# Feed-forward projections: one 512-column matmul for the high weights, and bank halves added on the way out

## The reference, cut to what matters

```
D_FF = 2816
def swiglu(x, w_gate, w_up, w_down):
    return (jax.nn.silu(x @ w_gate) * (x @ w_up)) @ w_down

h = rms_norm(x, g_pre)
x = x + rms_norm(swiglu(h, w_gate, w_up, w_down), g_post)      # stages 4 to 12: half of it for the feed-forward blocks
```

## Time and profile before

| | us |
|---|---|
| median of 3 runs | 2139.08 (2131.37 to 2140.52) |
| the profiled execution | 2141.63 |
| its span, first to last instruction | 2139.8 |
| PE busy | 2051.3 (96%) |
| DVE busy | 1389.2 (65%) |
| ACT busy | 944.5 (44%) |
| mean granted clock of TensorE | 0.974 of full |

### The profile page before, as it was taken

One profiled execution on the slowest core, in us unless ns is written; L12 is line 12 of the kernel. 1 busy time (PEld: TensorE's weight loads), 2 busy tenths in 40 slices (PEclk: granted clock), 3 DMA queues, 4 the chain that ended last, 5 costly groups with the idle time before them and its releaser, 6 DMA issues.

```text
span 2139.8 us, 37138 instructions
## 1 busy us (share of the span) xinstructions
PE 2051.3 (96%) x15066; PEld 1908.0 (89%) x15066; DVE 1389.2 (65%) x1853; ACT 944.5 (44%) x1258; POOL 33.0 (2%) x48
## 2 busy tenths in 40 slices
PE   7999999999999999999989989999999996999998
PEld 7879989999889989998988878998899895799997
DVE  6867756666757746765766555776577457565773
ACT  4544434444454434444353253444444343644442
POOL 0000000000000000000000010000000000000000
PEclk9999999999999999999998789999999998999999
DMA  7434554443425554554620133455455543142553
GB/s 291 148 128 177 196 206 169 176 151 145 141 107 196 189 205 156 188 205 164 227 74 1 60 126 130 159 195 207 156 193 185 205 181 128 50 158 109 193 193 115
DMA packets 49788, 341.46 MB, mean 160 GB/s; under 512 B 5776, under 2 KB 6544, under 8 KB 9616
## 3 DMA queue, kind: packets, MB, share of 16 engines
q1 hardware_dynamic: 45216, 321.21, 41.9%
q10 hardware_dynamic: 4464, 18.68, 2.4%
HBM read 338.82 MB, written 1.05 MB: 159 GB/s over the span
## 4 chain that ended last, share of the span: by engine, by line
PE 86%; DVE 9%; ACT 2%; issue 1%; POOL 0%; DMA 0%; DVEq 0%; SPq 0%; POOLq 0%; ACTq 0%
PE pj L229 15%; PE pj L228 15%; PE pj L230 15%; PE acc L234 7%; PE acc L236 7%; PE acc L235 7%; PE pj L234 2%; PE pj L235 2%; PE pj L236 2%; PE pj L567 2%; DVE wlo L304 2%; PE pj L573 1%; PE acc L633 1%; PE acc L646 1%; PE mb L657 1%
## 5 line engine op out<-in xcount | busy, mean ns | idle before, releaser
L304 DVE TENSOR_TENSOR wlo<-raw,whi 128x2048 fp32r<-128x2048 f32 x285 | 653.1, 2291 | 302.5 <-ACT whi L297 301.6
L228 PE MATMUL pj<-xh,whi 128*128 128x256 f32 x2704 | 760.6, 281 | 13.8 <-DVE wlo L314 13.3
L229 PE MATMUL pj<-xl,whi 128*128 128x256 f32 x2704 | 758.8, 281 | 0.0
L297 ACT ACTIVATE whi<-raw 128x2048 fp32r<-128x2048 f32 x299 | 569.9, 1910 | 425.2 <-PE acc L236 198.7
L230 PE MATMUL pj<-xh,wlo 128*128 128x256 f32 x2704 | 756.9, 280 | 0.0
L228 PEld LDWEIGHTS pj<-xh,whi 128*128 128x128 f32 x2704 | 511.1, 189 | 17.0 <-issue 15.8
L229 PEld LDWEIGHTS pj<-xl,whi 128*128 128x128 f32 x2704 | 510.1, 189 | 0.1
L230 PEld LDWEIGHTS pj<-xh,wlo 128*128 128x128 f32 x2704 | 508.8, 188 | 0.0
L234 PE MATMUL acc<-whi,AR 128*128 128x512 f32 x656 | 258.1, 394 | 6.7 <-DVE AR L2029 4.4
L235 PE MATMUL acc<-whi,AR 128*128 128x512 f32 x656 | 257.1, 392 | 0.0
L236 PE MATMUL acc<-wlo,AR 128*128 128x512 f32 x656 | 256.9, 392 | 0.0
(11 more groups left out here) (356 smaller groups left out, 2388.7 us busy)
## 6 DMA issues: line engine op xcount, KB each, us to landing
raw<-in_wstream SPq DMA_DIRECT2D x302, 1024.0 KB, 4.8
F<-in_gains ACTq DMA_DIRECT2D x12, 512.0 KB, 4.7
F<-in_rpb ACTq DMA_DIRECT2D x3, 1024.0 KB, 4.7
F<-in_memtok ACTq DMA_DIRECT2D x2, 1024.0 KB, 4.8
F<-in_memin ACTq DMA_DIRECT2D x2, 1024.0 KB, 6.9
F<-in_small ACTq DMA_DIRECT2D x1, 1536.0 KB, 10.7
F<-in_xin SPq DMA_DIRECT2D x2, 512.0 KB, 6.6
xt<-in_xtok SPq DMA_DIRECT2D x1, 1024.0 KB, 12.2
```

The lines of the kernel that those rows point to most:

```text
L228: nc.tensor.matmul(o, wh, k_hi, start=first, stop=False, skip_group_check=True)
L229: nc.tensor.matmul(o, wh, k_lo, start=False, stop=False, skip_group_check=True)
L297: nc.scalar.activation(whi[:, gs, :], raw[:, gs, :], ACT.Copy).then_inc(w_hi, 1)
L304: nc.vector.tensor_tensor(wlo[:, gs, :], raw[:, gs, :], whi[:, gs, :].bitcast(F32), ALU.subtract).then_inc(w_lo, 1)
```

## The change

The input's high and low parts `xh` and `xl` are laid next to each other in one tensor `xx`. For chunks 2 to 21 of a feed-forward stage, each tile of high weights now moves both in one matmul of 512 columns, and the low weights move the high input in one of 256: two matmuls and two weight loads a tile in place of three. The bank's left half then holds high by high plus low by high, the right half high by low. Gate and up need a whole bank each, so a chunk takes two banks (`pj` pairs, `acc[0]` and `acc[1]`, or a `pj` with `mb`, in turn). On the way out ACT copies the right halves to `GS` in SBUF (line 869 of the changed kernel, two instructions, counted by `ev`), DVE adds the left halves to them (line 834, two instructions), and then multiplies by `rP` (line 838, counted by `gu`).

The making of `wlo` is moved too: DVE no longer makes all of chunk c+3 in step c, but the two halves of chunk c+2, one before line 846 and one behind line 849 (805 and 808 before). Step c = 0 makes none. A whole one is added behind the last step.

```
         def tile_both(bank, half, slot):
+            for k in range(KT):
+                wk = slice((half * KT + k) * P, (half * KT + k + 1) * P)
+                nc.tensor.matmul(bank[:, :], whi[:, slot, wk], xx[:, k, :, :].rearrange("p a t -> p (a t)"),
+                                 start=k == 0, stop=False, skip_group_check=True)
+                last = nc.tensor.matmul(bank[:, 0:T], wlo[:, slot, wk], xh[:, k, :], start=False, stop=k == KT - 1,
+                                        skip_group_check=True)
+            return last

         # pe_f
-                proj_pe(pe, w, 1, tiles)
-                proj_pe(pe, w, FT - 3, tiles)
+                def body(c, g, gs, it, p, ps):
+                    k = (gs - w.g) % 3 + 2
+                    pe.wait_ge(w_lo, g + 1)
+                    pe.wait_ge(pj_free, p + 1 if not isinstance(c, int) or c != 1 else p + 2)
+                    two_ = banks(p0, k)
+                    tile_both(two_[0], 0, gs)
+                    if isinstance(c, int) and c == 0:
+                        pe.wait_ge(*at(tag + "pre", "rb", 1))
+                    tile_both(two_[1], 1, gs).then_inc(w_used, 1)
+                chunk_loop(pe, w, FT - 2, body, peel=2, is_proj=True)
+                pe.wait_ge(pj_free, 3 + w.p - 2)

         # dve_f, step c (c < 2 keeps the one multiply from the bank)
-                    dve_lo(dve, g, gs)
+                    else:
+                        dve.wait_ge(*at(tag, "ev", c - 1))
+                        for a, bank in enumerate(banks(p0, (gs - g0) % 3)):
+                            x = nc.vector.tensor_tensor(GS[:, a * T:(a + 1) * T], bank[:, 0:T],
+                                                        GS[:, a * T:(a + 1) * T], ALU.add)
+                        x.then_inc(pj_free, 1)
+                        dve.wait_ge(pj_free, p + 4)
+                        nc.vector.tensor_tensor(GU.rearrange("p (a t) -> p a t", a=2),
+                                                GS.rearrange("p (a t) -> p a t", a=2),
+                                                twice, ALU.mult).then_inc(sg(tag, "gu"), 1)
+                    before = not isinstance(c, int) or c > 0
+                    if before:
+                        dve.wait_ge(w_hi, g + 3)
+                        half_lo(dve, (gs - 1) % 3, 0)
                     dve.wait_ge(*at(tag, "th", c + 1))
...
+                    if before:
+                        half_lo(dve, (gs - 1) % 3, 1).then_inc(w_lo, 1)
                     dve.wait_ge(*at(tag, "hi2", c + 1))
...
                 chunk_loop(dve, w, FT, body, peel=2, is_proj=True)
+                dve_lo(dve, w.g - 1, (w.g - 1) % 3)

         # act_f, step c
+                    if not isinstance(c, int) or c > 1:
+                        act.wait_ge(w_used, g + 1)
+                        for a, bank in enumerate(banks(p0, (gs - g0) % 3)):
+                            x = nc.scalar.activation(GS[:, a * T:(a + 1) * T], bank[:, T:2 * T], ACT.Copy)
+                        x.then_inc(sg(tag, "ev"), 1)
```

More of the change, by code:

```diff
@@ L100, in build_program @@
                                            "od": groups}
-        ADDS = {"ffn": {n: FT for n in ("th", "a", "m", "hi2", "lo2")}, "na": {**attn(16, 8, 2), "oh": 8},
+        ADDS = {"ffn": {**{n: FT for n in ("th", "a", "m", "hi2", "lo2")}, "gu": FT - 2, "ev": FT - 2}, "na": {**attn(16, 8, 2), "oh": 8},
                 "dil": {**attn(16, 8, 2), "oh": 8, "pt": 32, "pts": 32}, "xa": {**attn(4, 4, 2), "oh": 4}, "dsa": attn(8, 8, 2), "rwrt": {}}
@@ L127, in build_program @@
         xt = sb("xt", [P, 2, D])
-        xh = sb("xh", [P, KT, T], F32R)
-        xl = sb("xl", [P, KT, T], F32R)
+        xx = sb("xx", [P, KT, 2, T], F32R)
+        xh, xl = xx[:, :, 0, :], xx[:, :, 1, :]
         sb("space", [P, 112])
@@ L250, in tile_fm, with tile_both @@
                     mid_tile.pop()()
+            return last
+        def tile_both(bank, half, slot):
+            for k in range(KT):
[4 more added lines that the diff above has]
+                                        skip_group_check=True)
             return last
@@ L781, in ffn @@
         def ffn(tag, s, nxt):
-            sh = FS - KT * T - 5 * T
+            sh = FS - KT * T - 7 * T
+            GS = F0[:, sh + 1280:sh + 1792]
             GU = F0[:, sh:sh + 512]
@@ L786, in ffn, with banks @@
             M = F0[:, sh + 1024:sh + 1280]
+            def banks(p0, c):
+                r = p0 % 3
+                return ((pj[r], pj[(r + 1) % 3]), (acc[0], acc[1]), (pj[(r + 2) % 3], mb))[c % 3]
             def pe_f(pe, w):
-                def tiles(c, j, bank, slot):
-                    tile_fm(bank, 0, slot)
-                    return tile_fm(bank, 1, slot)
+                p0 = w.p
                 slices_pe(pe, w)
-                proj_pe(pe, w, 1, tiles)
-                proj_pe(pe, w, FT - 3, tiles)
+                def body(c, g, gs, it, p, ps):
[9 more added lines that the diff above has]
+                pe.wait_ge(pj_free, 3 + w.p - 2)
@@ L795, in pe_f @@
                 out_pe(pe, w, FT, FT, tag, "lo2", nxt)
             def dve_f(dve, w):
+                p0, g0 = w.p, w.g
                 def body(c, g, gs, it, p, ps):
                     dve.wait_ge(w_used, g + 1)
-                    nc.vector.tensor_tensor(GU.rearrange("p (a t) -> p a t", a=2),
-                                            pj[ps][:, :].rearrange("p (a t) -> p a t", a=2),
-                                            rP[:, None, :].to_broadcast([P, 2, T]), ALU.mult).then_inc(pj_free, 1)
@@ L803, in body @@
-                    dve_lo(dve, g, gs)
+                    twice = rP[:, None, :].to_broadcast([P, 2, T])
+                    if isinstance(c, int) and c < 2:
+                        nc.vector.tensor_tensor(GU.rearrange("p (a t) -> p a t", a=2),
+                                                pj[ps][:, :].rearrange("p (a t) -> p a t", a=2),
+                                                twice, ALU.mult).then_inc(pj_free, 1)
+                    else:
[5 more added lines that the diff above has]
+                        dve.wait_ge(pj_free, p + 4)
+                        nc.vector.tensor_tensor(GU.rearrange("p (a t) -> p a t", a=2),
+                                                GS.rearrange("p (a t) -> p a t", a=2),
+                                                twice, ALU.mult).then_inc(sg(tag, "gu"), 1)
@@ L823, in body @@
                         act_hi(act, g + 1, (g + 1) % 3, (g + 1) // 3, c)
-                    act.wait_ge(pj_free, p + 4)
+                    if isinstance(c, int) and c < 2:
+                        act.wait_ge(pj_free, p + 4)
+                    else:
+                        act.wait_ge(*at(tag, "gu", c - 1))
                     nc.scalar.activation(TH, GU[:, 0:T], ACT.Tanh, scale=0.5).then_inc(sg(tag, "th"), 1)
```

## The result

The changed kernel takes 2163.4 us (median of four runs, 2160.03 to 2168.5) where the kernel before takes 2138.26 beside it: ratio 1.0123, interval 1.0101 to 1.0145. The forecast was 2159, so the sign and nearly the size came out. The profiled execution took 2160.03 us.

The account below looks back on a forecast made before the run. PE's stream and stops were taken to bound the kernel. Per stage -2.98 + 3.69 + 1.6 + 0.86 + 0.15 = +3.32 us, six stages +19.9, giving 2159 us; range 2144 to 2180.

Parts of the forecast that it names:

- The reading of what bounds the kernel: Whole kernel: PE, busy 96% of the span, sets the time by its stream's cost and where it stands still.
- Term 2: Start of chunk 3, each feed-forward stage: the moved `wlo` comes late and PE stands still for 3.69 us.
- term 1: PE's stream in feed-forward projections: merging saves a fixed share per tile, 0.149 us a chunk, -2.98 us a stage.
- Term 3: Behind the stop at chunk 3: PE's clock falls to half rate, +1.6 us a stage, bounds 0 and 1.8.
- Term 4: Loop through ACT and DVE after chunk 3: late `wlo` adds 0.045 us a chunk, +0.86 us a stage.
- X: Loop time from PE's going to chunk c+1 until it could start c+2: 5.60 us, bounds 5.40 to 6.0.
- C: PE's own time per chunk, 5.51 us; as rival: chunk 3's first `wlo` isn't late, 2121 us, chance 0.05.
- The sum: All terms plus 0.15 us for the second down chunk: +3.32 us a stage, +19.9 over six stages, 2159 us.
- A: Rival at chunk 3's stop: the clock stays up or falls only near its end, 2149.4 us, chance 0.13.
- B: Rival in the loop: slower, 6.0 us in place of 5.60, +22.8 us, 2182 us, chance 0.20.
- D: Rival in the projections: cheaper matmuls (5.36 us a chunk), loop 5.45, clock holds; 2132 us, no visible change, chance 0.07.

Follow-up runs that it names:

- move_alone: The kernel before, three matmuls a tile kept, with only `wlo` made in halves one step later as in the change: 2169.6 us, ratio 1.016.
- first_early: The changed kernel with chunk 3's `wlo` made whole in step 0, chunk 4's in step 1, none in step 2: 2144.23 us, ratio 1.0029.
- fill_seven: The changed kernel with 7 dummy matmuls on PE before the wait for chunk 3's `wlo`: 2155.85 us, ratio 1.0076.
- whole_lo: The changed kernel with the two `wlo` halves made as one instruction right behind the multiply by `rP`: 2157.74 us, ratio 1.0096.
- merge_alone: The kernel before with only PE's stream changed to 512 + 256 columns a tile, DVE and ACT in the old order: 2135.43 us, ratio 0.999.
- shifted: The changed kernel, started as first_early, then each `wlo` half made for a chunk half a turn later: 2137.4 us, ratio 0.9994.

## Why the forecast came out, step by step

**The reading of what bounds the kernel** held: PE's stream and its stops made all of the difference, DMAs and POOL none.

**Term 2, the late `wlo`, was exact.** The replay had chunk 3 at 160.47 + 9.20; it came 9.17 behind chunk 2. The stop reads 3.29, not 3.69, because chunk 2 itself took 0.20 more than the 5.51 of term 1 (the next start was due at 164.82) and because its last matmul counts as busy for 0.16 beyond that; the late start is the same. move_alone shows the same 9.26 with the old matmuls, and first_early takes it away by making the first two `wlo` a step earlier.

**Term 3, the clock, was in kind right and too small.** I took 1.6 us from one place, with 0 and 1.8 as bounds. At the stops it was 7.25 - 5.66 = 1.6 in three stages and 8.2 to 8.4 less 5.66 = 2.5 to 2.8 in three, where two neighbouring windows of 2 us stood at 0.50. In the mean 2.14, and fill_seven, in which the same stop is filled, measures 2.1 for a stage. The bound of 1.8 was the failed step: it came from the one stop of 4.39 us, and I took for granted that the low clock lasts as long everywhere. In both stops that I had from the trace of before, the clock fell only once PE had started again. For the one of 3.49 us the window 1112 to 1114 still has 1.00, and PE starts at 1113.55; for the one of 4.39 us it starts at 1247.96:

```profile
1246.00:1248.00 2.00, 0.04 (x1) 0.07 (x1) 1.93 (x6) 1.17 (x3) 0.00 (x0) 1.00 0.00 0
1248.00:1250.00 2.00, 2.00 (x5) 1.63 (x6) 0.82 (x3) 0.71 (x1) 0.00 (x0) 0.51 0.07 23
```

Over the changed kernel, move_alone and whole_lo, chunk 3 lost 1.6 us in each of the eight stages in which it was so. In the eight in which the clock fell while PE stood still, it lost 2.5 to 2.9 in six and 1.4 in two. Which of these a stop gets, no run here can set. A pair costs 0.64 at the half clock against 0.353, 1.8 times as much.

**Term 1, the merge, was the wrong step.** "What goes is one fixed share per tile": there is none. merge_alone has PE's 0.353 us a tile with two matmuls as with three, 117.8 ns for each 256 columns. What I took for an advantage of size in the down projection (226.4 ns for 512 columns, 442 ps a column, against 460) belongs to that stream, not to the size. The trace of before has 256-column matmuls at the same price, in the stretch between the first two feed-forward stages and at a granted clock of 1.00:

```profile
374.12 0.28 PE L228 MATMUL pj<-xh,whi 128*128 128x256 f32 x1
...
385.00 0.28 PE L234 MATMUL pj<-whi,xh 128*128 128x256 f32 x1
```

Between these two starts lie 96 matmuls of lines 228 to 230, with the input moving, at 113.3 ns each, and the 48 before them, with weights moving (from 368.66), take 113.6 ns each. Two of them cost what one 512 does. So I set a 512 of a quick stream against a 256 of a slow one. The bound "nothing, if a 512 with the input moving costs two of 256" was the right value. In some stretches there was 0.07 a chunk, half of the 0.149. The gap of 2.5 ns in the Trainium skill ("TensorE: Matmul & The Clock Gate", Back-to-back issue gap), which the page gives for a matmul by itself, would have saved 0.04 us a chunk; its sum was nearer to the measured 0 to 0.07 than the 0.149 from my rows, though its price for 256 columns (an estimate of 109 ns by that page) is below the 117.8 of the trace.

**Term 4, the loop, was right in kind.** In one step of the loop, on ACT, DVE and PE (182.12 is the start of the chunk on PE):

```profile
182.12 0.48 PE L257 MATMUL pj<-xx,whi 128*128 128x512 f32 x1
...
187.79 0.47 PE L257 MATMUL pj<-xx,whi 128*128 128x512 f32 x1
```

```profile
182.32 0.66 ACT L869 ACTIVATE F<-acc 128x256 f32<-128x256 f32 x2 [0.93 <-PE acc L259]
```

```profile
183.09 0.76 DVE L834 TENSOR_TENSOR F<-acc,F 128x256 f32<-128x256 f32 x2 [0.77 <-ACT F L869]
183.88 0.69 DVE L838 TENSOR_TENSOR F<-F,rP 128x512 f32<-128x512 f32 x1
184.49 1.22 DVE L320 TENSOR_TENSOR wlo<-raw,whi 128x1024 fp32r<-128x1024 f32 x1
...
186.41 1.22 DVE L320 TENSOR_TENSOR wlo<-raw,whi 128x1024 fp32r<-128x1024 f32 x1
```

These add up as follows: 0.20 to ACT, 0.66 for the two copies, 0.11 to DVE (forecast 0.03), 0.76, 0.03, 0.61, 1.13, 0.45, 0.34, 1.22 until 187.63, and 0.16 until PE: X = 5.67, against 5.60. Since C is 5.58 to 5.65 and not 5.51, PE's own stream is nearly as slow as the loop, and the chunks come at 5.66 in the mean. What the loop costs is 0.01 a chunk where C is 5.65. In stages that would run at 5.58 it hides that gain, at most 0.08 a chunk: shifted, without these waits, had one such stage (112.45 us), the changed kernel none.

**The sum.** For a stage, forecast and measured, against 113.16 us before: chunk 2 +3.54 and +3.51; chunk 3 +1.50 and +2.14; the other 18 chunks and the wait of the second down chunk -1.72 and 0.0; together +3.3 and +5.67. (X - 5.44 is 0.16, not the 0.15 of the forecast, which changes nothing.) The errors of terms 1 and 3 have one direction and, less what term 4 was too dear, come to 14 us over the six stages. The forecast of the total was nearer (2159 against 2163.4), because outside the projections the runs of the changed kernel took less time. In this the forecast was lucky: no run ties the 9 us between 34.0 and 25.1 to the change, and move_alone, with the same sum in the projections, took 2169.6.

**The rivals.** A (the clock holds) is refuted by the windows at 0.50 and by fill_seven. B (X = 6.0) is refuted by X = 5.67. C's premise (no late `wlo`) was made by experiment, and the result was not the 2121 of the rival but 2144 in first_early and 2137 in shifted, since term 1 isn't there. D needed a cheaper 512 and fails with term 1.

## What to carry to other kernels

When a helper engine's work is moved a step later in a pipelined loop, replay the first round: the steady state had room here, the peeled start had 1.81 us and lost 3.5. Count a stop of PE of this length with the low clock behind it, which cost here another 1.4 to 2.9 us for 3.3 to 3.4 of idleness. And price a merged matmul by its columns, not by the count of instructions, unless two streams that differ in nothing else show a fixed share; and look whether the smaller size has the better price anywhere in the same trace, as it had here.

## What the runs showed of the hardware that I hadn't expected

- 768 columns took 353.4 ns as three matmuls with three weight loads and as two with two. At the granted clock 0.50 they took 0.64 us, 0.83 ns a column, which is one column for each period of 1.2 GHz. At the full clock it is 0.46 ns a column, more than the 0.417 of a period of 2.4 GHz. So something other than the columns costs 10% there (6% in the streams at 113.3 ns for 256), and not at the low clock. What it is stays open.
- The same stream ran at 5.655 us a chunk in some stages and at 5.58 in others, at a granted clock of 1.00 in both; with another moving operand at 5.545 and 5.655. The kernel before has two prices too, 117.8 ns for 256 columns in the feed-forward projections and 113.3 in some chunks of the other stages. A stage keeps its rate throughout in merge_alone. The cause is open.
- After the same stop of 3.3 us chunk 3 lost 1.6 us to the low clock in three stages and 2.5 to 2.8 in the other three. It lost more where the clock fell before PE started again. A stop of 2.42 us brought the clock down in four of six stages; waits of 0.40 to 0.42 didn't.
- The plain fp32 constant of 256 columns showed as two rows and cost 0.43 us a matmul, 3.7 times the 0.118 of the kernel's own fp32r ones.
